# Score products cut by the causal quarter in a fused RWKV-7, windowed attention and convolution kernel

## The chip, the core and the metric

The kernel is one launch on one core of a Trainium2 chip. The metric is the device time of one execution in microseconds, median of three runs. Five engines work side by side and meet through semaphores: TensorE (PE in the profile; its weight loads are PEld), VectorE (DVE), ScalarE (ACT), GpSimd (POOL), and SyncE (SP), which issues most of the weight loads. PE reads SBUF and writes PSUM, which has eight banks of 2 KB per partition.

## What is computed

The reference is one layer: RMS norm, one projection `w_in`, an RWKV-7 recurrence over 16 heads of 64, an attention over windows of 128 with a sink, gates and projections, and a feed-forward part with a short convolution. The change lies in the recurrence:

```
def step(S, inp):
    r_t, w_t, k_t, v_t, aa_t, bb_t = inp
    sa = jnp.einsum('bhvk,bhk->bhv', S, aa_t)
    S = S * w_t[:, :, None, :] + sa[..., None] * bb_t[:, :, None, :] + v_t[..., None] * k_t[:, :, None, :]
    y_t = jnp.einsum('bhvk,bhk->bhv', S, r_t)
    return S, y_t
...
mean = jnp.mean(y, axis=-1, keepdims=True)
var = jnp.mean(jnp.square(y - mean), axis=-1, keepdims=True)
y = (y - mean) * lax.rsqrt(var + GN_EPS)
y = y.reshape(B, T, RWKV_DIM) * lnx_w.astype(f32) + lnx_b.astype(f32)
bonus = jnp.sum(rh * kh * r_k.astype(f32), axis=-1, keepdims=True) * vh
y = (y + bonus.reshape(B, T, RWKV_DIM)) * g.astype(f32)
```

T is 512 tokens. The step is linear in S, so the kernel works on chunks of 128 tokens with matrices of scores, which are zero where the key's token comes after the query's.

## The kernel before

The recurrence runs in eight **pairs** of heads, n = 0 to 7, 64 partitions for each head. Each engine has its instructions in an order written out by hand; semaphores with running counts join them. For one pair PE does, in this order:

- `scores`: per chunk j (four) and head h (two), one matmul with the 64x128 weights `bp` (the beta keys) or `kp` (the kappa keys) and the 256 columns of `ar` (alpha beside r) as moving operand. Every plain f32 matmul leaves two records in the trace, so each matrix has 16. Two chunks of one head fill one PSUM bank. VectorE's `masked` brings each bank to SBUF with a predicated copy through the triangle `causal`, to `gb` for the beta part and `gk` for kappa, and `g_ready` counts the eight copies. A memset of one column stands ahead of each copy and carries its wait.
- `norm_var(d)`, d = n-1: sums for the variance of the pair before, and its bonus rows. ScalarE takes the root (`deviation`, `std_ready`), PE turns it (`turned_var`), VectorE's `deviations` makes a reciprocal and spreads it over `ysq` (`vex_ready`), and PE turns that back (`turned(6, ysq)`, `rstd_ps`).
- `turned(2, ...)`, `turned(3, bp)` and `turned(1, kp)`: values, beta and kappa to token rows, in banks that earlier scores held.
- `invert`: the triangular system of each chunk and head is inverted by doubling, seven levels, 0 to 6. A level is a product on PE into v (`v_ps`), a masked copy on VectorE, a second product (`y_ps`) and an add on VectorE. It works on `n1`, ScalarE's f16 copy of the alpha columns of `gb` (`score_copy`), and VectorE starts `xx` from `n1` (`x_start`). GpSimd's `remainder` forms n2 = gb - n1, which is read after the last level.
- `scan(n)`: the state goes from chunk to chunk.

PE never has nothing to do: between these steps it takes **fillers**, three f32r matmuls of 512 columns each, of the gate and key projections. The tables `FILL`, `FILL_FIRST` and `FILL_LAST` say how many at which place ("scores", "centred", "tokens", (level, "masks") and so on). 24 fillers are three projection tiles per pair. Their weights are split in two on VectorE: `weights` (the whole tile, 1024 columns) and `weights_half` (512 columns, at levels 1, 2, 4 and 5).

GpSimd's queue in a pair: `bonus_product`, a store of gates, `odd_columns`, `remainder`, `bonus_back` (a store of `brow`, then two loads into z), `key_norms_in` (two loads of `kqn`, after `rstd_ps`), and the product of the loaded bonus with the values (`product_ready`, which VectorE wants at level 4). For pair 0 GpSimd also sets `gk` to zero once `ops_ready` says that the attention's scratch is free, and `cleared` counts that.

## Time and profile before

| what | us |
|---|---|
| median of three runs | 1024.72 (1024.06 to 1024.76) |
| the profiled execution | 1024.05 |
| its span | 1022.3 |
| PE busy in the span | 1011.7 |
| first scores, pair 0 | at 213.6 |
| last scores, pair 7 | at 498.1 |

Read it so: the pairs stand between 213.6 and about 525 us, each some 40.6 us long. The rest of the span is projection, attention and feed-forward work that the diff leaves alone. The granted PE clock is full speed in all 40 slices.

### The profile page before, as it was taken

To read this page: it belongs to the slowest core of one execution; us is meant where nothing else is said; L and a number is where in the kernel's file an instruction comes from. 1 tells how busy PE (TensorE), PEld (TensorE's weight loads), DVE (VectorE), ACT (ScalarE), POOL (GpSimd) and SP (SyncE) were. 2 spreads that over 40 slices of the span, in tenths; PEclk is the share of its full clock that TensorE was granted. 3 is DMA by queue.
4 is the path that set the end of the run, shared out by engine and by line. 5 is a ranking of instruction groups with operands and counts; after the bars stand their busy time and mean duration, and the time that the engine had idled before them with its cause. 6 is when DMAs were issued, how large, how long until landed. Compare 5 with 4: busy or idle time off the path is not lost.

```text
span 1022.3 us, 18746 instructions
## 1 busy us (share of the span) xinstructions
PE 1011.7 (99%) x7106; PEld 806.3 (79%) x7106; DVE 738.1 (72%) x1233; ACT 516.2 (50%) x869; POOL 224.4 (22%) x298
## 2 busy tenths in 40 slices
PE   8999999999999999999999999999999999999997
PEld 7888888777777777777777888888888888888886
DVE  5224667788988888888877565367767777789786
ACT  6435756844435445345453322264455444467744
POOL 7642355330221422413210554000000000000000
PEclk9999999999999999999999999999999999999999
DMA  6874456331303313214255867613233333337662
GB/s 187 233 236 153 132 191 215 94 76 43 86 25 74 86 63 87 61 60 120 93 164 153 238 234 258 198 40 103 85 102 92 95 100 103 92 114 226 203 189 113
DMA packets 161291, 133.25 MB, mean 130 GB/s; under 512 B 32729, under 2 KB 137735, under 8 KB 161223
## 3 DMA queue, kind: packets, MB, share of 16 engines
q1 hardware_dynamic: 147687, 88.41, 29.7%
q0 software_dynamic: 13520, 43.90, 13.9%
q8 instruction: 47, 0.77, 0.3%
q14 instruction: 21, 0.17, 0.0%
q10 hardware_dynamic: 16, 0.00, 0.0%
HBM read 111.83 MB, written 20.45 MB: 129 GB/s over the span
## 4 chain that ended last, share of the span: by engine, by line
PE 94%; DVE 2%; DMA 1%; issue 1%; ACT 1%; POOL 0%; SPq 0%; DVEq 0%; POOLq 0%; ACTq 0%
PE ps L2090 14%; PE ps L2093 14%; PE ps L2092 14%; PE ps L2046 6%; PE ps L2048 5%; PE ps L2047 5%; PE ps L2677 3%; PE ps L2678 3%; PE ps L2679 3%; PE ps L2291 3%; PE ps L2425 2%; PE ps L2232 2%; PE ps L2613 1%; PE ps L2611 1%; PE ps L2612 1%; PE ps L2374 1%
## 5 line engine op out<-in xcount | busy, mean ns | idle before, releaser
L1357 DVE TENSOR_TENSOR wlo<-raw,whi 128x1024 fp32r<-128x1024 f32 x106 | 140.1, 1322 | 125.9 <-ACT whi L893 108.0
L893 ACT ACTIVATE whi<-raw 128x1024 fp32r<-128x1024 f32 x116 | 122.6, 1057 | 127.0 <-PE ps L2093 116.0
L2090 PE MATMUL ps<-xnh,whi 128*128 128x512 f32 x336 | 130.7, 389 | 0.0
L2092 PE MATMUL ps<-xnl,whi 128*128 128x512 f32 x336 | 130.7, 389 | 0.0
L2093 PE MATMUL ps<-xnh,wlo 128*128 128x512 f32 x336 | 130.7, 389 | 0.0
L2046 PE MATMUL ps<-xh,whi 128*128 128x512 f32 x192 | 89.5, 466 | 0.0
L2090 PE MATMUL ps<-xh,whi 128*128 128x512 f32 x224 | 88.3, 394 | 0.0
L2092 PE MATMUL ps<-xl,whi 128*128 128x512 f32 x224 | 87.3, 390 | 0.0
L2093 PE MATMUL ps<-xh,wlo 128*128 128x512 f32 x224 | 87.2, 389 | 0.0
L2048 PE MATMUL ps<-xh,wlo 128*128 128x512 f32 x192 | 76.1, 396 | 0.0
L2047 PE MATMUL ps<-xl,whi 128*128 128x512 f32 x192 | 75.3, 392 | 0.0
L2090 PEld LDWEIGHTS ps<-xnh,whi 128*128 128x128 f32 x336 | 63.1, 188 | 13.2
L2092 PEld LDWEIGHTS ps<-xnl,whi 128*128 128x128 f32 x336 | 63.1, 188 | 13.2
L2093 PEld LDWEIGHTS ps<-xnh,wlo 128*128 128x128 f32 x336 | 63.1, 188 | 13.0
L1093 ACT ACTIVATE xx<-ps 128x256 f16<-128x256 f32 x96 | 32.1, 381 | 69.1 <-PE ps L2331 68.3
L2090 PEld LDWEIGHTS ps<-xh,whi 128*128 128x128 f32 x224 | 42.0, 188 | 10.1 <-issue 0.8
L2093 PEld LDWEIGHTS ps<-xh,wlo 128*128 128x128 f32 x224 | 42.1, 188 | 8.9
L2092 PEld LDWEIGHTS ps<-xl,whi 128*128 128x128 f32 x224 | 42.1, 188 | 8.4
L1879 DVE TENSOR_TENSOR sq<-ps,rs 128x512 f32<-128x512 f32 x44 | 30.4, 691 | 23.5 <-PE ps L2093 18.5
L745 POOL TENSOR_TENSOR z<-z,kmod 128x512 f32<-128x512 f32 x8 | 16.2, 2025 | 126.2 <-DVE kp L1488 126.2
L2048 PEld LDWEIGHTS ps<-xh,wlo 128*128 128x128 f32 x192 | 36.0, 188 | 8.3
L1608 DVE TENSOR_TENSOR yy<-ps,yy 128x256 f16<-128x256 f32 x96 | 36.2, 419 | 8.6 <-PE ps L2374 8.3
(430 smaller groups left out, 2454.6 us busy)
## 6 DMA issues: line engine op xcount, KB each, us to landing
raw<-in_w_in SPq DMA_DIRECT2D x108, 256.0 KB, 3.3
raw<-in_w_up SPq DMA_DIRECT2D x88, 256.0 KB, 3.0
wrow<-in_w_down POOLq DMA_DIRECT2D x22, 512.0 KB, 5.1
raw<-weight_scratch SPq DMA_DIRECT2D x44, 256.0 KB, 3.4
raw<-in_w_down SPq DMA_DIRECT2D x32, 256.0 KB, 2.9
weight_scratch<-wrow POOLq DMA_DIRECT2D x11, 512.0 KB, 3.1
gates_scratch<-gst POOLq DMA_DIRECT2D x16, 256.0 KB, 3.2
raw<-in_w_proj_b SPq DMA_DIRECT2D x16, 256.0 KB, 4.2
```

What stands on the lines that cost most here:

```text
L893: act.activation(flat(whi[:, hb]), flat(raw[:, b]), ACT.Copy).then_inc(w_hi, 1)
L1093: act.activation(dst, src, ACT.Copy).then_inc(x_ready, 1)
L1357: dve.tensor_tensor(flat(lo[:, hb]), flat(raw[:, b]), flat(hi[:, hb]).bitcast(F32), ALU.subtract).then_inc(w_lo, 1)
L1608: dve.tensor_tensor(yg, low_half(ps[2 * g][:, :], lv), yg, ALU.add)\
L2046: pe.matmul(o, whi[:, hb, k, :], self.hi(k), start=k == 0, stop=False)
L2047: pe.matmul(o, whi[:, hb, k, :], self.lo(k), start=False, stop=False)
L2048: ins = pe.matmul(o, wlo[:, hb, k, :], self.hi(k), start=False, stop=k == KT - 1)
L2090: pe.matmul(ps[bank][:, :], whi[:, hb, k, :], hi(k), start=first and k == 0, stop=False)
L2092: pe.matmul(ps[bank][:, :], whi[:, hb, k, :], lo(k), start=False, stop=False)
L2093: ins = pe.matmul(ps[bank][:, :], wlo[:, hb, k, :], hi(k), start=False, stop=last and k == kn - 1)
L2291: ins = pe.matmul(ps[SCORE_BANK[f + h]][:, (j - j0) * 2 * C: (j - j0 + 1) * 2 * C], src[hs, j * C:(j + 1) * C], ar[hs, 1 - n % 2, j, :], s ...
L2677: pe.matmul(o, h_hi, hi[:, cols], start=start, stop=False)
```

## The change

The matrices of scores of a chunk are cut in the middle of the token axes. Keys 0 to 63 against queries 0 to 63 are the **early** quadrant; the columns of queries 64 to 127 are the **late** half, for all 128 keys. The quadrant of late keys and early queries is zero and is left out.

- PE: 16 early matmuls with 64x64 weights and 128 columns; even chunks land in the upper 64 partitions of the bank, odd ones in the lower. Then 16 late matmuls with 64x128 weights and 128 columns. The banks are 2 and 3 for early, 0, 1, 4 and 5 for late.
- VectorE: four early copies of 64 partitions for both matrices at once, with one memset ahead of the first, two late copies of beta, the centring of the values (`value_tokens`), two late copies of kappa. `gb` and `gk` become views of one tile, `gg`. In pair 0 the early copies wait for `cleared` 2, since they write both.
- `turned_var` goes behind the turning of values and beta. The filler at "scores" is gone and "centred" has two. `deviations` moves into `invert`: on VectorE behind the level 0 copies, on PE behind the first product of level 1.
- ScalarE's `score_copy` waits for six copies in place of four.
- GpSimd: `bonus_back` goes ahead of `remainder`, and `remainder` waits for `x_start` too.

```diff
+EARLY_BANK = (2, 3)
+LATE_BANK = ((0, 1), (4, 5))
...
+        gg = take("gg", [P, NT, 2, 2, 2, C])
+        gb, gk = (gg[:, 2 * i:2 * i + 2].rearrange("p x e h q t -> p (x e) h (q t)")
+                  for i in range(2))
...
             def remainder(n):
                 pool.wait_ge(n1_ready, n + 1)
+                pool.wait_ge(x_start, n + 1)
...
                 odd_columns(n)
+                bonus_back(n - 1)
                 remainder(n)
-                bonus_back(n - 1)
...
             def score_copy(n):
-                act.wait_ge(g_ready, n * 8 + 4)
+                act.wait_ge(g_ready, n * 8 + 6)
...
+            def early_masked(n, h, e):
+                if n == 0:
+                    dve.wait_ge(cleared, 2)
+                dve.wait_ge(g_ps, n * 8 + 4)
+                predicated(gg[0:HD, :, e, h, :, 0:C // 2],
+                           two_parts(causal[0:HD, :], slice(0, C // 2)),
+                           ps[EARLY_BANK[h]][e * HD:(e + 1) * HD, :]
+                           .rearrange("p (x q t) -> p x q t", x=NT, q=2),
+                           None if h or e else 0)
...
+                    if lv == 0 and d is not None:
+                        deviations(d)
...
-                for f in range(6):
-                    masked(n, f)
-                deviations(n - 1)
-                for f in range(6, 8):
-                    masked(n, f)
+                masked(n, 0)
                 value_tokens(n)
+                masked(n, 1)
                 invert(n, n - 1, n < PAIRS - 1)
...
+                for i, src in enumerate((bp, kp)):
+                    for jj in range(2):
+                        o = (2 * i + jj) * C
+                        for e in range(2):
+                            j = 2 * jj + e
+                            for h, hs in enumerate(rows):
+                                ins = pe.matmul(ps[EARLY_BANK[h]][e * HD:(e + 1) * HD, o:o + C]
+                                                .rearrange("p (q t) -> p q t", q=2),
+                                                src[hs, j * C:j * C + HD], both(hs, j, slice(0, HD)),
+                                                start=True, stop=True)
+                                if i and jj:
+                                    ins.then_inc(g_ps, 1)
+                late(0)
+                late(1)
                 if d is not None:
                     norm_var(d)
-                fill("scores")
-                if d is not None:
-                    turned_var(d)
-                pe.wait_ge(g_ready, n * 8 + 3)
+                pe.wait_ge(g_ready, n * 8 + 2)
                 turned(2, z[:, n + 16, :]).then_inc(tok_ps, 1)
                 pe.wait_ge(g_ready, n * 8 + 4)
                 turned(3, bp).then_inc(tok_ps, 1)
                 if d is not None:
-                    deviations(d)
+                    turned_var(d)
                 fill("centred")
-                pe.wait_ge(g_ready, n * 8 + 8)
+                pe.wait_ge(g_ready, n * 8 + 6)
                 turned(1, kp).then_inc(tok_ps, 1)
...
+                    if lv == 1 and d is not None:
+                        deviations(d)
                     fill((lv, "masks"))
```

PE's order at the start of a pair's scores, before (`gb,up` is the end of the pair before, `z,rkcols` the bonus sums):

```order
L2291 MATMUL ps<-ar,bp 128x256 [waits ops_ready]
L2291 MATMUL ps<-ar,bp 128x256 x7
L2291 MATMUL ps<-ar,kp 128x256 x4
L2291 MATMUL ps<-ar,kp 128x256 [waits g_ready]
L2291 MATMUL ps<-ar,kp 128x256 x3
L2226 MATMUL ps<-ysq,meancols 32x128 [waits y_scaled,ysq_ready]
```

And now:

```order
L2331 MATMUL ps<-ar,bp 64x128 [waits ops_ready]
L2331 MATMUL ps<-ar,bp 64x128 x7
L2331 MATMUL ps<-ar,kp 64x128 x8
L2318 MATMUL ps<-ar,bp 128x128 x8
L2318 MATMUL ps<-ar,kp 128x128 x8
L2251 MATMUL ps<-ysq,meancols 32x128 [waits y_scaled,ysq_ready]
```

Twice the matmuls, each of half the columns, and no wait inside them.

VectorE's order at the end of the copies and the start of the inversion, before (`n_95` is `n1`, `v_96` is `v1`):

```order
L1532 COPY_PREDICATED gk<-causal,ps 128x2x256
L1520 RECIPROCAL ystd<-ps 128x8 [waits std_ps]
L1507 COPY ysq<-ystd 128x512 [waits dve_chain]
L1531 MEMSET carrier 128x1 [waits g_ps]
L1532 COPY_PREDICATED gk<-causal,ps 128x2x256
L1531 MEMSET carrier 128x1 [waits g_ps]
L1532 COPY_PREDICATED gk<-causal,ps 128x2x256
L1497 TENSOR_REDUCE vsum<-ps 128x8 [waits tok_ps]
L1499 SCALAR_TENSOR_TENSOR vp<-vsum,ps 128x512 [waits dve_chain]
L1582 TENSOR_TENSOR xx<-n_95,first_level 128x1024 [waits n1_ready,rk_product]
L1597 TENSOR_TENSOR yy<-ps,level_mask 128x256 [waits v_ps] x2
L1597 TENSOR_TENSOR v_96<-ps,level_mask 128x128x2 [waits v_ps] x2
```

And now:

```order
L1502 SCALAR_TENSOR_TENSOR vp<-vsum,ps 128x512 [waits dve_chain]
L1531 MEMSET carrier 128x1 [waits g_ps]
L1532 COPY_PREDICATED gg<-causal,ps 128x4x2x64
L1531 MEMSET carrier 128x1 [waits g_ps]
L1532 COPY_PREDICATED gg<-causal,ps 128x4x2x64
L1608 TENSOR_TENSOR xx<-n_95,first_level 128x1024 [waits n1_ready,rk_product]
L1623 TENSOR_TENSOR yy<-ps,level_mask 128x256 [waits v_ps] x2
L1523 RECIPROCAL ystd<-ps 128x8 [waits std_ps]
L1510 COPY ysq<-ystd 128x512 [waits dve_chain]
L1623 TENSOR_TENSOR v_96<-ps,level_mask 128x128x2 [waits v_ps] x2
```

The reciprocal and the spread copy stood ahead of the last two copies of kappa, and now stand behind `xx` and the level 0 copies.

GpSimd's order in the same pair, before:

```order
L752 COPY yy<-ident 128x512 [waits ops_ready]
L738 TENSOR_TENSOR n_97<-gb,n_95 128x1024 [waits n1_ready]
L814 DMA bonus_scratch<-brow 128x128 [waits std_ready]
L817 DMA z<-bonus_scratch 64x4x128 [waits brow_stored]
L817 DMA z<-bonus_scratch 64x4x128
L808 DMA kqn<-key_scratch 64x4x128 [waits rstd_ps]
L808 DMA kqn<-key_scratch 64x4x128
L850 TENSOR_TENSOR z<-z 128x512 [waits bonus_in]
```

And now:

```order
L755 COPY yy<-ident 128x512 [waits ops_ready]
L817 DMA bonus_scratch<-brow 128x128 [waits std_ready]
L820 DMA z<-bonus_scratch 64x4x128 [waits brow_stored]
L820 DMA z<-bonus_scratch 64x4x128
L741 TENSOR_TENSOR n_97<-gg,n_95 128x1024 [waits x_start,n1_ready]
L811 DMA kqn<-key_scratch 64x4x128 [waits rstd_ps]
L811 DMA kqn<-key_scratch 64x4x128
L853 TENSOR_TENSOR z<-z 128x512 [waits bonus_in]
```

The subtraction (`n_97`, which is n2) moved behind the three bonus transfers and has a second wait.

## Rows read from the trace of the kernel before

**Rows 1.** The page: busy time of each engine, share of the span, instructions.

```profile
PE 1011.7 (99%) x7106; PEld 806.3 (79%) x7106; DVE 738.1 (72%) x1233; ACT 516.2 (50%) x869; POOL 224.4 (22%) x298
```

**Rows 2.** Timeline, PE, pair 5: start us, us, engine, line, operation, shapes, count.

```profile
416.86 2.00 PE L2291 MATMUL ps<-ar,bp 64*128 64x256 f32 x16
...
420.54 0.42 PE L2226 MATMUL ps<-ysq,meancols 128*32 128x128 f32 x8
420.79 0.40 PE L2226 MATMUL ps<-z,rkcols 128*32 128x128 f32 x8
...
422.95 0.66 PE L2232 MATMUL ps<-ident,ysq 128*128 128x128 f32 x4
423.37 0.48 PE L2046 MATMUL ps<-xh,whi 128*128 128x512 f32 x1
...
428.41 0.41 PE L2374 MATMUL ps<-v,xx 128*128 128x64 f16 x8
...
430.71 0.41 PE L2374 MATMUL ps<-v,xx 128*128 128x64 f16 x8
```

**Rows 3.** Timeline, PE, a score product of the attention stage.

```profile
84.36 1.16 PE L2176 MATMUL ps<-kb,qc 64*128 64x128 f32 x16
```

**Rows 4.** Timeline, DVE, pair 5.

```profile
418.03 0.75 DVE L1532 COPY_PREDICATED gb<-causal,ps 128x512 f32<-128x512 uint32 x1 [0.29 <-issue]
418.66 0.76 DVE L1532 COPY_PREDICATED gb<-causal,ps 128x512 f32<-128x512 uint32 x1
...
422.47 0.43 DVE L1507 COPY ysq<-ystd 128x512 f32<-128x512 f32 x1
...
424.13 0.66 DVE L1497 TENSOR_REDUCE vsum<-ps 128x8 f32<-128x512 f32 x1
...
425.43 0.69 DVE L1582 TENSOR_TENSOR xx<-n,first_level 128x1024 f16<-128x1024 f16 x1
426.03 0.78 DVE L1597 TENSOR_TENSOR yy<-ps,level_mask 128x256 f16<-128x256 f32 x2
...
429.41 0.68 DVE L1569 TENSOR_TENSOR wlo<-raw,whi 128x512 fp32r<-128x512 f32 x1
430.01 0.75 DVE L1597 TENSOR_TENSOR v<-ps,level_mask 128x256 f16<-128x256 f32 x2
```

**Rows 5.** Timeline, POOL, pair 5.

```profile
422.82 2.15 POOL L738 TENSOR_TENSOR n<-gb,n 128x1024 f16<-128x1024 f32 x1 [2.65 <-ACT n L1073]
...
427.01 1.26 POOL L817 DMA_DIRECT2D z<-bonus_scratch  x2 [1.55 <-DMA bonus_scratch<-brow]
428.26 1.25 POOL L808 DMA_DIRECT2D kqn<-key_scratch  x2
...
432.60 1.29 POOL L850 TENSOR_TENSOR z<-z 128x512 f32<-128x512 f32 x1 [3.09 <-DMA z<-bonus_scratch]
```

**Rows 6.** Timeline, pair 0, POOL and DVE.

```profile
215.26 1.88 POOL L829 MEMSET gk<- 128x2048 f32 x1
...
220.43 2.17 POOL L738 TENSOR_TENSOR n<-gb,n 128x1024 f16<-128x1024 f32 x1
...
221.67 1.49 DVE L1582 TENSOR_TENSOR xx<-n,first_level 128x1024 f16<-128x1024 f16 x1
```

**Rows 7.** Timeline, late in the attention stage, POOL and DVE.

```profile
187.93 1.81 POOL L797 MEMSET gb<- 128x2048 f32 x1 [0.89 <-ACT vc L983]
...
188.57 1.19 DVE L1414 TENSOR_SCALAR nmx<-mx 128x8 f32<-128x8 f32 x1
```

**Rows 8.** Timeline, pair 0 and pair 1: PE and DVE.

```profile
218.95 0.60 PE L2232 MATMUL ps<-ident,bp 128*128 128x128 f32 x4
...
253.87 2.00 PE L2291 MATMUL ps<-ar,bp 64*128 64x256 f32 x16
...
255.33 0.74 DVE L1532 COPY_PREDICATED gb<-causal,ps 128x512 f32<-128x512 uint32 x1
...
265.69 0.41 PE L2374 MATMUL ps<-v,xx 128*128 128x64 f16 x8
```

63 lines of the change are left out of this document (36 added, 27 removed).

## The prediction

> **What bounds the kernel now.** First the page: PE is busy 1011.7 of 1022.3 us [rows 1]. Nothing else comes near, so the kernel gets shorter only where PE has less work, and longer by every wait put into PE's queue. Then the timeline of one pair, since the other seven repeat it. I take pair 5, count from its first score product at 416.86, and call that zero. The scores last until the variance sums at 420.54, 3.68 us; the level 1 update (L2374) starts at 428.41, so at 11.55 [rows 2]. All that the diff moves lies between these two marks or hangs on VectorE's and GpSimd's queues in that stretch [rows 4, 5]. So I ask when the level 1 update starts now. PE has a filler at almost every place, and the fillers keep their number; a wait that outlasts them is lost for good.
>
> **PE's own work.** Before: 32 score records, 3.68 us [rows 2]. Late: 32 records of 128 columns in the form of the attention's product, 16 in about 1.0 to 1.16 us [rows 3], so some 2.0 us. Early: 32 records of 128 columns on quarters of the array. No row shows a 64x64 product. The nearest is the variance sum, also 128 columns and four parts of the array side by side: 8 records in 0.25 us (420.54 to 420.79) [rows 2], so 32 in 1.0 us. If two run at a time and not four, they cost half of today's scores, 1.84 us. I take 1.0, by the row with four parts at work. Scores then last 3.0 to 3.1 us, 0.6 us less in each of eight pairs. The merged filler saves one start, about 0.1 us. If PE waited for nobody, this would be worth 8 x 0.7 = 5.6 us. It does wait, as follows.
>
> **VectorE's chain.** The first early copy needs all early products. The last group of 8 begins at 0.75 and ends 0.42 later, at 1.17; the copy follows 0.24 us on, as I read the 418.03 start behind the first products. So it starts at 1.41 (now 1.17) [rows 2, 4]. The eight copies have as many elements as before. Copies start 0.63 us apart (418.03, 418.66) and take 0.75 each [rows 4]. The four early ones read partitions 0 and 64 in turn with no memset between; no row has that, so their step lies between 0.63 (overlapped as now) and 0.75 (one after another), and I take the middle, 0.69, as no row is nearer to either. Two late copies of 0.63 and 0.65, the two steps of `value_tokens` 1.30 (424.13 to 425.43), two more copies 1.28 [rows 4]: `xx` starts at 1.41 + 2.76 + 1.28 + 1.30 + 1.28 = 8.03 and ends 0.69 later, at 8.72. It started at 8.57 before. The three memsets that fall away are 0.06 us each and lie under the copies: nothing.
>
> On this step the Trainium skill has a rule, in "VectorE: DVE Perf Modes", section "Two Vector instructions with no wait between them": an instruction whose input starts in another group of 32 partitions than the last one read there is held until the earlier ones have finished. By it the step would be the long one; by the rows alone it is open. No run here shows it yet.
>
> **Where it turns: the spread copy meets the subtraction.** `deviations` now stands behind `xx` and the level 0 copies, and PE takes its result at level 1. GpSimd's `remainder` (2.15 us) [rows 5] now waits for `x_start`, so it starts just as `xx` ends: 8.72 + 0.08 = 8.80, until 10.95. The level 0 copies start 0.60 after `xx`, last 0.67, then the reciprocal 0.24; the spread copy wants to start at 9.54, in the middle of the subtraction. Can they run together? Two rows say no. In pair 0 `xx` took 1.49 us and not 0.69, beside the same subtraction, which ended at 222.60; `xx` ended at 223.16 [rows 4, 6]. And a VectorE instruction with one input, 8 elements wide, took 1.19 us and ended at 189.76, when GpSimd's memset ended at 189.74 [rows 7]. The spread copy moves 512 f32 elements in 0.43 us, where a predicated copy of as many takes 0.75 [rows 4]: it runs in a faster mode, the kind of instruction I expect to be shut out. It would then end about 0.30 after the subtraction (as `xx` did, 0.13 less than its length), at 11.25. PE's turning of `ysq` starts at 11.30, then 0.42 to the filler's start (422.95 to 423.37) and 0.79 for the filler: the level 1 update starts at 12.51 and not at 11.55 [rows 2]. PE's own path would have brought it to the turning at about 9.6: it stands still for 1.7 us, more than all that the scores save.
>
> The skill's page "SBUF — State Buffer", section "Who interferes with whom", gives the reason and names the class: a copy of f32 from SBUF to SBUF can take the port pair shared with GpSimd, and the second to issue blocks fully until the first is done. The two rows above agree with it, 1.49 and 1.19 us; for this very copy no row shows it.
>
> Cost: pairs 3 to 7, 0.96 each, 4.8 us. In pairs 1 and 2 VectorE has one more instruction and started its copies at 255.33 - 253.87 = 1.46 already; their update stood at 265.69 - 253.87 = 11.82 [rows 8] and goes to 12.56: 0.74 each, 1.5 us.
>
> **A second collision.** `key_norms_in` waits for `rstd_ps`, which the turning at 11.30 gives at 12.0. Its two transfers take 1.25 [rows 5], then the bonus product (1.29) runs from 13.3 to 14.6. Its data are there: the loads into z are issued from about 6.5 and the product started 5.6 after that issue (427.01 to 432.60) [rows 5], so at 12.1. VectorE's first half split of weights starts 1.00 after the update (428.41 to 429.41) [rows 2, 4], at 13.5, and has two SBUF inputs, as `xx` has. It would be shut out until 14.6 and end at 15.15 in place of 14.2. The level 2 masks behind it come 0.95 late; level 2's update, which stands 0.70 behind their start (430.01 to 430.71) with nothing to spare, moves by about 0.9. That hits pairs 1 to 6, 5.4 us; pair 7 has no key norms to load. The order of the two is a matter of 0.2 us, so this term is the least sure. Bounds: 0 and 0.95 a pair.
>
> **Pair 0.** Its early copies wait until GpSimd has cleared `gk`, 215.26 + 1.88 = 217.14 [rows 6]; before, the first copy needed only `gb`. The fourth copy then ends at 217.2 + 3 x 0.69 + 0.75 = 220.0, and PE turns beta at 220.1 in place of 218.95 [rows 8], with one filler (0.8) still to come that stood ahead of it. Cost 1.9 us; with steps of 0.63, 1.7. ScalarE's score copy is later too, but PE meets it behind three fillers. In this pair `xx` gains, 0.69 for 1.49, hidden under the fillers of level 0.
>
> **GpSimd's order.** Bonus rows go some 3.7 us earlier and are wanted at level 4: nothing. n2 ends at 10.95, wanted after level 6: nothing. ScalarE's copy for `n1` ends near 6.8 for a filler that PE reaches at about 6.7: a few hundredths, and inside the wait at the turning.
>
> **Sum.** 4.8 + 1.5 + 5.4 + 1.9 = 13.6 us. The profiled execution was 1024.05 with a span of 1022.3, so 1.75 us lie outside the span, untouched; it stands 0.67 below the median. 1024.72 + 13.6 = **1038.3 us**.
>
> **The rivals.**
> 1. *Blocked, but no second collision.* The half split starts before the product and GpSimd waits. 13.6 - 5.4 = 8.2: 1032.9; with steps of 0.63, 1031. For it: the order is decided by 0.2 us. Chance 0.22.
> 2. *The spread copy runs beside the subtraction.* Then the turning follows VectorE's own chain, 9.54 + 0.43 + 0.05 = 10.02, the update stands at 11.23: 0.32 less than before in five pairs, 0.54 less in two, 1.9 lost in pair 0, so -0.8: 1023.9. With steps of 0.63 the update comes 0.24 earlier and pair 0 loses 1.7: -2.7, **1022.1, faster**. It decides from where the spread copy takes its usual 0.43 us in pairs 1 to 7. For it: no row shows a spread copy beside GpSimd, and its source is a broadcast; against it, the two blocked rows. Chance 0.15, half of it faster, half within 0.2%.
> 3. *Quarters of the array run two at a time.* The first early copy then starts 0.84 later, all behind it too, except in pair 0, which waits for GpSimd anyway: about +5.8, 1044.1. Against it: four parts are at work in the variance sums. Chance 0.07.
> 4. Something else that I don't see, either way: 0.06.
>
> The forecast itself has 0.50. **Range**: the steps of 0.75 add 1.9, to 1040.2, and a part of rival 3 goes to 1043; below, rival 1 with short steps is 1031, and between it and rival 2 lie mixtures (blocked in part, or rival 2 with the second collision), so I go down to 1026. A difference of 0.2%, 2 us, is about what a measurement can tell here. Faster: half of rival 2 and a third of the last case, 0.09. Same: 0.09. Slower: 0.82.
>
> **What the changed profile will show.** Early records of x32 in about 1.0 us, scores 3.0 to 3.1 us long, each pair. The spread copy (L1510) at 1.5 to 1.7 us in place of 0.43, ending with GpSimd's subtraction (L741), and PE's turning of `ysq` right behind it; if it stands at 0.43, rival 2 holds. Half splits (L1595) of 1.5 us in pairs 1 to 6; if all are 0.68, rival 1. In pair 0 the first early copy at 217.2 with PE idle before it. `xx` at 0.69 in all pairs. PE's busy time should fall or stay while the span grows. I am wrong altogether if PE reaches the level 1 update sooner than 11.5 us after its first score product.

## The result and the profile after

| | before | after |
|---|---|---|
| median, us | 1024.74 (4 runs, 1024.06 to 1025.93) | 1045.16 (4 runs, 1043.99 to 1049.69) |
| span of the profiled execution, us | 1022.3 | 1043.6 |
| its own time, us | 1024.05 | 1045.36 |
| ratio | | 1.0209, interval 1.0197 to 1.0222 |

The change makes the kernel 2.1% slower, 20.4 us. Direction and mechanism are those of the prediction; the forecast of 1038.3 was 6.9 us too low, and the measured time lies above the range that ended at 1043. So does the fastest execution of after, 1043.99 us with a granted clock of 1.000 over its span; the slowest, 1049.69, had 0.989.

The page of after, the lines that answer to [rows 1]:

```profile
span 1043.6 us, 19242 instructions
PE 1012.1 (97%) x7362; PEld 808.3 (77%) x7362; DVE 755.0 (72%) x1209; ACT 516.9 (50%) x869; POOL 225.1 (22%) x298
```

PE's busy time is the same (1011.7 before), and the span is 21.3 us longer. So PE stands still now. What it waits for, after, in the view of PE's waits (engine and line, what released it, us in total, times, longest us), the three longest but for a load at the start:

```profile
PE ps L2257 <- DVE ysq L1510: 12.4, 7, 2.1
PE ps L2415 <- DVE v L1623: 4.2, 6, 0.8
PE ps L2257 <- DVE gg L1532: 3.4, 4, 2.0
```

None of the three was in the trace of before. The first is the turning of the spread copy, seven times; the second is the level 2 update behind a late half split; the third is mostly pair 0. Now pair 5, where the first score product stands at 430.27. Timeline, PE, after:

```profile
430.27 0.67 PE L2331 MATMUL ps<-ar,bp 64*64 64x128 f32 x16
...
433.29 0.43 PE L2251 MATMUL ps<-ysq,meancols 128*32 128x128 f32 x8
...
439.86 0.41 PE L2390 MATMUL ps<-yy,n 128*128 128x64 f16 x8
441.97 0.66 PE L2257 MATMUL ps<-ident,ysq 128*128 128x128 f32 x4 [1.70 <-DVE ysq L1510]
...
443.17 0.41 PE L2415 MATMUL ps<-v,xx 128*128 128x64 f16 x8
...
446.43 0.62 PE L2415 MATMUL ps<-v,xx 128*128 128x64 f16 x8 [0.81 <-DVE v L1623]
```

The last line once more in two narrow windows, since it is two groups of four, one for each of the two mask copies:

```profile
446.43 0.29 PE L2415 MATMUL ps<-v,xx 128*128 128x64 f16 x4 [0.81 <-DVE v L1623]
...
446.76 0.29 PE L2415 MATMUL ps<-v,xx 128*128 128x64 f16 x4
```

Timeline, DVE, after, same pair:

```profile
431.53 0.72 DVE L1532 COPY_PREDICATED gg<-causal,ps 64x512 f32<-64x512 uint32 x1 [0.38 <-issue]
...
432.28 2.28 DVE L1532 COPY_PREDICATED gg<-causal,ps 64x512 f32<-64x512 uint32 x3
...
438.48 0.68 DVE L1608 TENSOR_TENSOR xx<-n,first_level 128x1024 f16<-128x1024 f16 x1
...
439.97 1.95 DVE L1510 COPY ysq<-ystd 128x512 f32<-128x512 f32 x1
...
444.17 1.86 DVE L1595 TENSOR_TENSOR wlo<-raw,whi 128x512 fp32r<-128x512 f32 x1
445.96 0.74 DVE L1623 TENSOR_TENSOR v<-ps,level_mask 128x256 f16<-128x256 f32 x2
```

The second of these two masks in a narrow window:

```profile
446.29 0.41 DVE L1623 TENSOR_TENSOR v<-ps,level_mask 128x256 f16<-128x256 f32 x1
```

Timeline, POOL, after, same pair:

```profile
438.21 1.25 POOL L820 DMA_DIRECT2D z<-bonus_scratch  x2 [2.84 <-DMA bonus_scratch<-brow]
439.48 2.14 POOL L741 TENSOR_TENSOR n<-gg,n 128x1024 f16<-128x1024 f32 x1
...
442.93 1.24 POOL L811 DMA_DIRECT2D kqn<-key_scratch  x2 [1.30 <-PE ps L2257]
444.17 1.30 POOL L853 TENSOR_TENSOR z<-z 128x512 f32<-128x512 f32 x1
```

Read the three together. The spread copy, 0.43 us before [rows 4], takes 1.95 and ends at 441.92, 0.30 behind GpSimd's subtraction (441.62). PE has nothing left from 440.27 on and turns `ysq` at 441.97. The half split, 0.68 before [rows 4], starts in the same hundredth as the bonus product, takes 1.86 and ends at 446.03, 0.56 behind it. The update of level 2 comes 3.26 behind that of level 1, where it was 2.30 [rows 2]. It also takes 0.62 in place of 0.41: its first four products start 0.06 behind the first mask (446.37), and the other four wait for the second mask, which ends at 446.70. Before, PE came to the update only when the first mask had been ready for 0.28 us, and the second wait hardly showed. The summary of the spread copy's line over the whole of after (duration in ns, least, median and most; first and last start) says that seven of eight were like this, and the one behind the last pair was not:

```profile
L1510 DVE COPY ysq<-ystd x8: 426/1992/2348, 267.3 to 564.7; 128x512 f32<-128x512 f32 x8
```

The 21.3 us by pair, from the first score product of a pair to that of the next (pair 7: to its last update):

| pair | before | after | more | of it at the level 1 update | at level 2 | at level 3 |
|---|---|---|---|---|---|---|
| 0 | 40.23 | 43.78 | 3.55 | 3.55 | 0 | 0 |
| 1 | 40.86 | 43.11 | 2.25 | 1.07 | 0.97 | 0.21 |
| 2 | 40.89 | 43.43 | 2.54 | 1.35 | 0.96 | 0.22 |
| 3 | 40.62 | 42.94 | 2.32 | 1.19 | 0.96 | 0.22 |
| 4 | 40.62 | 43.36 | 2.74 | 1.58 | 0.96 | 0.22 |
| 5 | 40.64 | 43.14 | 2.50 | 1.35 | 0.96 | 0.21 |
| 6 | 40.62 | 43.90 | 3.28 | 1.73 | 1.57 | 0 |
| 7 | 23.99 | 26.11 | 2.12 | 1.58 | 0.34 | 0.21 |

The columns add up to 13.4, 6.7 and 1.3 us; the forecast had 8.2 (1.9 + 1.5 + 4.8), 5.4 and nothing. The last two columns are one loss: the first is what the first half of the level 2 update lost, and the second what its other half lost on top, behind the second mask. Together they are 1.17 to 1.18 us in pairs 1 to 5.

Pair 0. Timeline, PE, after:

```profile
218.72 0.66 PE L2257 MATMUL ps<-ident,z 128*128 128x128 f32 x4 [1.99 <-DVE gg L1532]
220.24 0.81 PE L2257 MATMUL ps<-ident,bp 128*128 128x128 f32 x4 [0.86 <-DVE gg L1532]
220.70 0.77 PE L2071 MATMUL ps<-xh,whi 128*128 128x512 f32 x1
221.27 0.63 PE L2072 MATMUL ps<-xl,whi 128*128 128x512 f32 x1
221.69 0.63 PE L2073 MATMUL ps<-xh,wlo 128*128 128x512 f32 x1
```

Windows of after (start:end, length, busy us of PE, of its weight loads, of DVE, ACT and POOL, then PEclk, the granted clock as a share of 2.4 GHz, the DMA engines' share, GB/s):

```profile
218.00:225.00 7.00, 5.42 (x22) 4.37 (x23) 6.60 (x14) 2.35 (x3) 2.52 (x6) 0.76 0.49 74
...
484.00:492.00 8.00, 6.50 (x62) 4.86 (x63) 6.40 (x11) 2.46 (x5) 3.68 (x4) 0.79 0.48 56
```

Beta is turned at 220.24, 6.59 behind the first score product where it was 5.31 [rows 8], as forecast (220.1; the copies wait for the memset). But the filler products that follow start 0.57 and 0.42 apart and not 0.23: TensorE ran at its lower level, 1.2 GHz, until about 224, after two stretches of idle time, 1.99 and 0.86 us. In before the same window had a clock of 1.00. Pair 6 shows the same after a wait of 2.10 us: 0.79 in its window, 1.00 before. Pairs 4 and 7, with waits of 1.94 and 1.92 us, show no filler at the lower level.

### The profile page after: what moved, and what is told of

The parts are those of the page before. It is cut to its first block, busy times and chain, and to the rows that moved or that the text cites. A ratio compares the mean times of both kernels' runs of the same rounds, so it can differ in the third digit from the quotient of the medians.

```text
span 1043.6 us, 19242 instructions
## 1 busy us (share of the span) xinstructions
PE 1012.1 (97%) x7362; PEld 808.3 (77%) x7362; DVE 755.0 (72%) x1209; ACT 516.9 (50%) x869; POOL 225.1 (22%) x298
## 3 DMA queue, kind: packets, MB, share of 16 engines
q0 software_dynamic: 13520, 43.90, 14.4%
## 4 chain that ended last, share of the span: by engine, by line
PE 84%; DVE 10%; issue 3%; DMA 1%; ACT 1%; POOL 0%; SPq 0%; DVEq 0%; POOLq 0%; ACTq 0%
PE ps L2115 14%; PE ps L2117 14%; PE ps L2118 14%; PE ps L2071 5%; PE ps L2073 4%; PE ps L2072 4%; PE ps L2718 3%; PE ps L2720 3%; PE ps L2719 3%; DVE gg L1532 2%; DVE ysq L1510 1%; PE ps L2415 1%; PE ps L2653 1%; PE ps L2654 1%; PE ps L2652 1%
## 5 line engine op out<-in xcount | busy, mean ns | idle before, releaser
L1532 DVE COPY_PREDICATED gg<-causal,ps 64x512 f32<-64x512 uint32 (+1 forms) x64 | 45.6, 735 | 4.8 <-issue 1.9
L2118 PEld LDWEIGHTS ps<-xh,wlo 128*128 128x128 f32 x224 | 42.0, 188 | 8.9
L1636 DVE TENSOR_TENSOR yy<-ps,yy 128x256 f16<-128x256 f32 x96 | 36.2, 419 | 13.4 <-PE ps L2415 12.6
```

What stands on the lines that cost most here:

```text
L1532: dve.copy_predicated(dst, mask.bitcast(U32).unsqueeze(1) .to_broadcast([mask.shape[0], NT, 2, C // 2]), scores)\
L1636: dve.tensor_tensor(yg, low_half(ps[2 * g][:, :], lv), yg, ALU.add)\
L2118: ins = pe.matmul(ps[bank][:, :], wlo[:, hb, k, :], hi(k), start=False, stop=last and k == kn - 1)
```

## The experiments

Three questions were open. Is it the meeting on the two engines' time line that makes the spread copy and the half split long, or the copy's new place, or the split of the copies? What does each cost? And what is the rest of pair 0? In the rows of an experiment the line numbers are its own. Kernels that ran together share the runs of the kernel before, whose median lay between 1024.41 and 1024.74 each time.

### Only GpSimd held back: `gate_only`

```diff
-                remainder(n)
                 if n < PAIRS - 1:
                     pool.wait_ge(rstd_ps, n)
                     key_norms_in(n + 1)
+                pool.wait_ge(w_half, 2 * n + 1)
                 pool.wait_ge(bonus_in, 32 * n)
                 pool.tensor_tensor(z[:, n + 7, :], z[:, n + 15, :], z[:, n + 7, :], ALU.mult)\
                     .then_inc(product_ready, 1)
+                pool.wait_ge(w_lo, N_FILL + 3 * n + 2)
+                remainder(n)
```

> The changed kernel with GpSimd alone held back: the bonus product waits until the first half split of level 2 is done, and the subtraction stands behind the product and waits for the third split, so that neither runs while VectorE spreads 1/std or makes the first half split. The split copies, the late spread copy and pair 0 stay as in the change. Theory (the two collisions between GpSimd and the spread copy and half split are the loss of pairs 1 to 7): spread copy 0.43 instead of 1.75 to 2.35, half splits 0.68 instead of 1.25 to 1.86, level 1 update at 11.3 to 11.6 (now 12.7 to 13.3), pairs 1 to 6 at 40.4 to 40.9 (now 42.9 to 43.9), pair 0 unchanged at 43.8; whole 1026 to 1029. Rival (the extra late copies and the spread copy's late place lengthen VectorE's own chain, and the collisions only fill time that it would wait anyway): pairs stay above 42, whole above 1037.

Measured: 1027.16 us (10 runs, 1025.24 to 1028.73), ratio 1.0027 [1.0017, 1.0036]; span 1024.2. The expected time, and the expected rows but for two: pair 0 took 42.23 and not 43.8 (its clock did not fall, see further down), and the second half split, at level 2, met the product in pairs 4 to 7 and took 0.80 to 1.30. Timeline, DVE, `gate_only`, pair 5 (first score product at 418.80):

```profile
428.50 0.43 DVE L1512 COPY ysq<-ystd 128x512 f32<-128x512 f32 x1
...
431.19 0.68 DVE L1597 TENSOR_TENSOR wlo<-raw,whi 128x512 fp32r<-128x512 f32 x1
```

Timeline, POOL, `gate_only`:

```profile
432.54 1.28 POOL L853 TENSOR_TENSOR z<-z 128x512 f32<-128x512 f32 x1 [1.37 <-DMA z<-bonus_scratch]
434.45 2.14 POOL L741 TENSOR_TENSOR n<-gg,n 128x1024 f16<-128x1024 f32 x1 [0.63 <-DVE wlo L1597]
```

Waits of PE, `gate_only`:

```profile
PE ps L2259 <- DVE ysq L1512: 1.3, 7, 0.2
```

Nothing of PE's or VectorE's work was touched, and 18.0 us are gone; by the two traces 19.4, of which 1.55 is the clock in pair 0. PE's wait for the spread copy falls from 12.4 to 1.3 us, pairs 1 to 6 take 40.4 to 40.8. The two collisions are the loss of pairs 1 to 7: shown. This kernel also answers for pair 0, further down.

### The spread copy back at its early place: `dev_early`

```diff
                 masked(n, 0)
+                deviations(n - 1)
                 value_tokens(n)
                 masked(n, 1)
                 invert(n, n - 1, n < PAIRS - 1)
...
-                    if lv == 0 and d is not None:
-                        deviations(d)
```

> One edit: VectorE's reciprocal and spread copy go back ahead of the centring of the values, where GpSimd has no computing instruction; PE still turns ysq at level 1. Shared way into SBUF: the copy takes 0.43 us again, xx starts 0.65 later, PE waits at most 0.4 us for the level 0 copies, and the half split of level 1 starts before the bonus product: about 2.4 us a pair less, 1028. Chain on VectorE alone: the work on VectorE is the same, so the time stays near 1045.

Measured: 1032.37 us (1031.68 to 1033.15), ratio 1.0076 [1.0059, 1.0092]; span 1030.7. All spread copies take 0.43 us, and the level 1 update stands at 11.6 to 11.8 behind the first score product. GpSimd's subtraction still stands behind `xx` and disturbs nothing now. The second collision came and went with the place of the product. Timeline, DVE, `dev_early`, pair 3:

```profile
354.97 2.22 DVE L1595 TENSOR_TENSOR wlo<-raw,whi 128x512 fp32r<-128x512 f32 x1
```

Timeline, POOL, `dev_early`, pair 3:

```profile
355.33 1.31 POOL L853 TENSOR_TENSOR z<-z 128x512 f32<-128x512 f32 x1
```

In pairs 1 and 3 the half split took 2.22 us and ended 0.55 behind the product (pairs of 42.36 and 42.18); in pair 2 the product began 0.65 behind its start, in pairs 4 to 6 more than 0.9, and those pairs took 40.6 to 40.8. So a product a few tenths of a microsecond earlier or later costs 1.5 us or nothing.

### GpSimd's order as before: `undo_pool`

```diff
                 pool.wait_ge(n1_ready, n + 1)
-                pool.wait_ge(x_start, n + 1)
...
-                bonus_back(n - 1)
                 remainder(n)
+                bonus_back(n - 1)
```

> One edit: GpSimd's part undone, the subtraction again ahead of the bonus transfers and without its wait for x_start. Shared way into SBUF: now xx is shut out by about 0.6 us, the spread copy is free at 0.43, and the bonus product comes long after the half split of level 1: 2 us a pair less, about 1030. If instead the splitting of the scores itself costs the time, it stays near 1045.

Measured: 1031.49 us (1030.63 to 1032.7), ratio 1.0064 [1.0047, 1.0081]; span 1031.0. Timeline, DVE, `undo_pool`, pair 5:

```profile
432.10 1.36 DVE L1607 TENSOR_TENSOR xx<-n,first_level 128x1024 f16<-128x1024 f16 x1
...
434.28 0.43 DVE L1509 COPY ysq<-ystd 128x512 f32<-128x512 f32 x1
```

Timeline, POOL, `undo_pool`:

```profile
430.76 2.15 POOL L740 TENSOR_TENSOR n<-gg,n 128x1024 f16<-128x1024 f32 x1 [3.58 <-ACT n L1075]
```

The subtraction is ahead of the spread copy again, which takes 0.43; now `xx` is the one that is shut out, 1.36 us in place of 0.69, until 0.55 behind the subtraction. That is why the change holds the subtraction back: the split makes `n1` ready earlier, and the subtraction would sit beside `xx`. But 0.7 us there cost less than 1.5 at the spread copy. All half splits take 0.68.

### Both back, only the split copies left: `split_alone`

The two edits above together.

> The changed kernel with both of these undone (VectorE's spread copy early again, GpSimd's order and wait as before): the split of the scores and what hangs on it alone. No instruction is shut out for longer than 0.2 us, the half splits are all 0.68; pairs 1 to 7 take 40.6 us as before, though PE has 0.65 us less work in each, since VectorE's copies decide when level 1 can start. What is left above 1024.7 is pair 0, 3.5 to 4.7 us: 1028 to 1030. If PE's smaller work comes through, 1024.

Measured: 1030.12 us (1028.14 to 1031.02), ratio 1.0044 [1.003, 1.0058]; span 1029.3. Pairs 3 to 6 take 40.77 to 40.81, 0.15 to 0.19 longer than before although the scores are 0.65 us shorter: VectorE's chain gives the gain back (PE's waits for the level 0 copies: 2.5 us in seven pairs). There are eight copies a pair as before, but the first starts 0.09 later, four of the steps are long (`copy_order`, below), and `xx` takes 0.80 in place of 0.68, since it starts before the subtraction ends. What each of these costs alone was not measured. Pair 0 takes 45.04. The split of the products alone brings nothing and costs 4.8 us in pair 0, clock included.

### The two moves, each alone, in the kernel before

`pool_on_before` (GpSimd's bonus transfers first, the subtraction held until `xx`):

```diff
                 pool.wait_ge(n1_ready, n + 1)
+                pool.wait_ge(x_start, n + 1)
...
-                remainder(n)
                 bonus_back(n - 1)
+                remainder(n)
```

> The kernel before with GpSimd's part of the change alone (bonus transfers first, the subtraction after xx). The spread copy stands ahead of xx there, so nothing on VectorE that wants the shared way runs beside the subtraction. Collision theory: the time stays at 1024.7 within 2 us, unless the bonus product, now earlier, meets the half split of level 1 (then up to 6 us more). If the new order of GpSimd is dear in itself, through its later subtraction, about 10 us more.

Measured: 1024.41 us (10 runs), ratio 1.0000 [0.9991, 1.001]; span 1022.6. No change: the spread copy sits ahead of the subtraction, 0.43 us long. The product meets the half split here too, but it is the product that waits. Timeline, POOL, `pool_on_before`, pair 5 (the half split runs from 429.79 for 0.68):

```profile
426.64 2.14 POOL L739 TENSOR_TENSOR n<-gb,n 128x1024 f16<-128x1024 f32 x1 [0.84 <-DVE xx L1583]
...
429.99 1.64 POOL L851 TENSOR_TENSOR z<-z 128x512 f32<-128x512 f32 x1
```

`dev_on_before` (only the spread copy and PE's turning of it moved; the first two pieces are VectorE's, the last two TensorE's):

```diff
+                    if lv == 0 and d is not None:
+                        deviations(d)
...
-                for f in range(6):
+                for f in range(8):
                     masked(n, f)
-                deviations(n - 1)
-                for f in range(6, 8):
-                    masked(n, f)
...
-                if d is not None:
-                    deviations(d)
                 fill("centred")
...
+                    if lv == 1 and d is not None:
+                        deviations(d)
                     fill((lv, "masks"))
```

> The kernel before with the move of the reciprocal and spread copy alone (VectorE behind the level 0 copies, PE at level 1); GpSimd's order as before. The subtraction is over by 8.1 us of the pair, the spread copy comes at about 9: it takes 0.43 us, and the time stays within 2 us of 1024.7. If the move is dear in itself, because PE waits for a longer chain, 5 us or more above.

Measured: 1022.23 us (10 runs, 1021.73 to 1023.24), ratio 0.9976 [0.9966, 0.9985]; span 1020.4. A gain of 2.4 us, the best kernel of all. Timeline, DVE, `dev_on_before`, pair 5 (first score product at 416.00):

```profile
423.60 1.05 DVE L1582 TENSOR_TENSOR xx<-n,first_level 128x1024 f16<-128x1024 f16 x1
...
425.46 0.43 DVE L1507 COPY ysq<-ystd 128x512 f32<-128x512 f32 x1
```

Timeline, POOL, `dev_on_before`:

```profile
421.94 2.15 POOL L738 TENSOR_TENSOR n<-gb,n 128x1024 f16<-128x1024 f32 x1 [2.63 <-ACT n L1073]
```

The spread copy is off the chain that leads to `xx`, so the level 1 update comes at 11.20 and not 11.55 [rows 2]. The subtraction ends at 424.09, ahead of the copy: they don't meet. It meets `xx` instead (1.05 in place of 0.69), and the pair gains even so. Of the two halves of the move one is worth nothing alone and the other 2.4 us; in the changed kernel, together, they put the two instructions side by side. Both together in the kernel before were not run.

### The product ahead of the key norms: `prod_first`

```diff
+                pool.wait_ge(bonus_in, 32 * n)
+                pool.tensor_tensor(z[:, n + 7, :], z[:, n + 15, :], z[:, n + 7, :], ALU.mult)\
+                    .then_inc(product_ready, 1)
                 if n < PAIRS - 1:
                     pool.wait_ge(rstd_ps, n)
                     key_norms_in(n + 1)
-                pool.wait_ge(bonus_in, 32 * n)
-                pool.tensor_tensor(z[:, n + 7, :], z[:, n + 15, :], z[:, n + 7, :], ALU.mult)\
-                    .then_inc(product_ready, 1)
```

> One edit: the bonus product goes ahead of the key norm loads on GpSimd. Shared way into SBUF: in pairs 1 to 3, whose bonus rows land early, the half split of level 1 is 0.68 us again and not 1.86; in pairs 4 to 6, whose store of bonus rows takes 3 us, the product still meets it in part. About 4.5 us less, 1040. If the long half split has another cause (its weights, PE), its length stays 1.86 us and the time 1045.

Measured: 1041.52 us (1040.64 to 1042.27), ratio 1.0167 [1.015, 1.0184]; span 1038.9. In pairs 1 to 3 the level 2 update is back at 2.30 behind that of level 1, and the pairs take 1.15 to 1.2 us less than in after. In pairs 4 to 6 it is not. There the z loads wait 2.7 to 3.4 us for the bonus rows' store (3.36 in pair 5), and the product then waits another 2.0 to 2.3 for the loads to land, so it still starts only 0.60 and 0.31 us ahead of the half split in pairs 4 and 6. In these two the first half of level 2 is still 0.3 and 0.6 us late; in pair 5 the spread copy takes 2.46 us, PE idles for 2.21, and the next filler products start 0.58 and 0.43 apart, at the lower clock. Right for three pairs of six.

### One reciprocal out of PSUM in place of reciprocal and spread copy: `psum_recip`

```diff
-                chain(dve.reciprocal(by_token(ystd[:, :]), by_token(ps[6][:, P:2 * P])))
-                spread(ysq, ystd).then_inc(vex_ready, 1)
+                dve.reciprocal(ysq[:, :].rearrange("p (j h v) -> p j h v", j=NT, v=HD),
+                               by_token(ps[6][:, P:2 * P]).unsqueeze(3)
+                               .to_broadcast([P, NT, 2, HD])).then_inc(vex_ready, 1)
```

> One edit to the changed kernel: VectorE's reciprocal and spread copy become one reciprocal of 512 elements that reads PSUM and no SBUF; GpSimd's queue is untouched. If the spread copy is shut out by GpSimd's subtraction because both want the shared way into SBUF, the new instruction takes about 0.7 us beside the subtraction, PE's idle of 1.5 to 2.1 us ahead of turning ysq shrinks to about 0.3, and the time falls from 1045 by 10 us or more, to about 1034; the half split may then come ahead of the bonus product and free up to 6 us more (1028). If the wait at the turning is only a long chain on VectorE, the time stays within 2 us of 1045.

Measured: 1061.3 us (1059.62 to 1062.32), ratio 1.0352 [1.0335, 1.037]; span 1060.6. Timeline, DVE, `psum_recip`, pair 1:

```profile
312.12 3.35 DVE L1523 RECIPROCAL ysq<-ps 128x512 f32<-128x512 f32 x1
```

The expected 0.7 us was a miss. The operation takes 3.33 to 3.35 us in all seven pairs, though GpSimd's subtraction (2.1 us) runs beside it in each, and 3.35 behind the last pair, where GpSimd does nothing. So this operation, which reads PSUM, is not shut out at the very place where the spread copy is; but it is dearer than the blocked copy, and PE waits 22.9 us for it. The time says nothing about the theory, the lengths do.

### Pair 0: fillers ahead of the first wait, `p0_fill`

```diff
                 if d is not None:
                     norm_var(d)
+                fill("scores")
                 pe.wait_ge(g_ready, n * 8 + 2)
...
-            FILL_FIRST = {**FILL, "centred": 3, (3, "update"): 1}
+            FILL_FIRST = {**FILL, "scores": 3, "centred": 0, (3, "update"): 1}
```

> Only in pair 0: the three fillers stand ahead of the first wait for a copy (ahead of value head's turning) instead of behind the beta turnings. Nothing else of the changed kernel is touched. Theory (pair 0 lost 3.55 us: 1.9 of it idle time of TensorE behind the late memset, the rest because its granted clock fell after that idle time and everything to 225 ran at the lower level): the fillers cover 0.7 us of the idle stretch with work; if that keeps the clock at 1.00 in 218 to 225, pair 0 takes 42.0 to 42.4 instead of 43.78 and the whole 1043.4 to 1043.8; pairs 1 to 7 keep their 42.9 to 43.9. Rival (all 3.55 us are waits for VectorE and the clock is without effect): pair 0 shortens by at most the 0.7 us of the three fillers that stood behind the wait, 43.1, whole 1044.5 or more.

Measured: 1045.19 us (1044.27 to 1045.48), ratio 1.0197 [1.0182, 1.0213]; span 1043.8. Pair 0 takes 43.42, not 42.0 to 42.4. The times are on the rival's side (43.1 or more, 1044.5 or more), but they don't speak for it, since the clock fell here too. The long idle stretch is gone, but three shorter ones take its place, and the granted clock is 0.89 in 218 to 225, with the low level from 223.4 to 226.7. Timeline, PE, `p0_fill`:

```profile
220.94 0.66 PE L2257 MATMUL ps<-ident,bp 128*128 128x128 f32 x4 [0.83 <-DVE gg L1532]
222.34 0.66 PE L2257 MATMUL ps<-ident,kp 128*128 128x128 f32 x4 [0.74 <-DVE gg L1532]
223.43 0.80 PE L2071 MATMUL ps<-xh,whi 128*128 128x512 f32 x1 [0.43 <-ACT n L1076]
```

The price of the clock came out of `gate_only`, whose pair 0 has the change's edits and the same waits of PE, and in whose profiled execution the clock did not fall. Timeline, PE, and window, `gate_only`:

```profile
219.30 0.66 PE L2259 MATMUL ps<-ident,z 128*128 128x128 f32 x4 [1.99 <-DVE gg L1534]
220.81 0.66 PE L2259 MATMUL ps<-ident,bp 128*128 128x128 f32 x4 [0.86 <-DVE gg L1534]
```

```profile
218.00:225.00 7.00, 4.84 (x33) 3.84 (x33) 6.84 (x15) 2.79 (x4) 2.98 (x5) 1.00 0.54 100
```

Its pair 0 takes 42.23: 2.0 us more than before, where the prediction had 1.9. With the clock at 0.76 (after) it takes 43.78, and in `dev_early`, `undo_pool` and `split_alone`, at 0.63, 0.61 and 0.69, it takes 44.89, 44.99 and 45.04. PE's waits for the early copies add up to 3.4 us in each of these. So the waits cost 2.0 us of the pair, and the clock 1.5 to 2.8 on top. The same kernel doesn't pay it in every execution: over the ten runs of `gate_only` the mean clock of the span goes from 0.999 (1025.24 us) down to 0.996 (1028.73 us). What decides it from run to run stays open.

### The order of the early copies: `copy_order`

```diff
-                    for h in range(2):
-                        for e in range(2):
+                    for e in range(2):
+                        for h in range(2):
                             early_masked(n, h, e)
...
-                pe.wait_ge(g_ready, n * 8 + 2)
+                pe.wait_ge(g_ready, n * 8 + 3)
```

> The changed kernel with its four early masked copies in the order head 0 and head 1 of one operand, then of the other, in place of both operands of head 0 first; TensorE's first turning waits for the third copy. Theory (a copy that starts on other partitions than the one before takes the longer step, 0.76 us, one on the same partitions 0.63): if the step hangs on a change of start partition alone, the order changes the last three steps' sum of 2.28 us by -0.1 to -0.25 and the subtraction xx starts that much earlier; the whole moves by less than 1.5 us, 1043.7 to 1045.2, since the turning waits for the spread copy behind GpSimd's subtraction, and not for xx. Rival (the step of 0.76 is that of every pair of copies that follow each other at once): 2.28 unchanged, whole 1045.2 within 0.5. Against both: pair 0 may lose 0.7 us more, since its first turning then waits for one copy more.

Measured: 1044.28 us (1043.86 to 1045.62), ratio 1.0195 [1.018, 1.0211]; span 1042.2. Timeline, DVE, `copy_order`, pair 5:

```profile
430.71 0.73 DVE L1532 COPY_PREDICATED gg<-causal,ps 64x512 f32<-64x512 uint32 x1 [0.38 <-issue]
...
431.35 2.11 DVE L1532 COPY_PREDICATED gg<-causal,ps 64x512 f32<-64x512 uint32 x3
```

The first copy and the second write and read the same partitions, and their step is 0.64; in after they change partitions, and the step is 0.75. The next three take 2.11 in place of 2.28. In both kernels every step to another start partition is 0.74 to 0.79, the one from the last early copy to the first late one too, and the others are 0.62 to 0.66. So it is the change of start partition that makes a step long, as expected. Pairs 1, 2, 3 and 5 are 0.26 to 0.31 shorter, the others scatter with the collisions; the whole can't be told from after at this precision.

### Everything mended, and once too much: `tuned1` and `tuned2`

`tuned1` is `gate_only`, `p0_fill` and `copy_order` in one, with pair 0's two late beta copies made ahead of its early ones, since they don't need the memset; TensorE's first two turnings then wait for the fifth and sixth copy there:

```diff
             def masked(n, i):
+                if n == 0 and i == 0:
+                    for h in range(2):
+                        late_masked(n, 0, h)
```

> The changed kernel with GpSimd put where it meets nothing: bonus product behind the half split of level 1, subtraction behind the half split of level 2; early copies in the order of partitions 0, 0, 64, 64; in pair 0 the late beta copies ahead of the early ones and three fillers ahead of the first wait. Collision theory: spread copy 0.43, half splits 0.68, level 1 update at about 11.2 of the pair and not 12.9, pair 0 costs 0.5 to 1 us and not 3.6, PE's clock stays up: 1022 to 1023, faster than both kernels. If something else holds the pairs back, it stays above 1028.

Measured: 1022.92 us (10 runs, 1021.9 to 1023.96), ratio 0.9981 [0.9971, 0.999]; span 1021.8. Pair 0 takes 40.54 (before 40.23, after 43.78) with the clock at 1.00; pairs 1 to 3 take 40.16 to 40.37, pairs 4 to 6 40.27 to 40.63, where the second half split met the product (1.05 to 1.37 us). The changed kernel's layout with GpSimd kept out of the way is 0.2% faster than before, at the edge of what can be told; it does not beat the simple `dev_on_before`.

`tuned2` moves one wait of it:

```diff
-                pool.wait_ge(w_half, 2 * n + 1)
+                pool.wait_ge(w_half, 2 * n + 2)
```

> The last mended version with one wait moved: the bonus product waits for the second half split of level 2 in place of the first. Theory (in pairs 4 to 6 of that version the second half split took 1.15 instead of 0.68 us because the product ran beside it, and levels 2 and 3 came 0.15 to 0.5 us late): half splits all 0.68, pairs 4 to 6 at 40.15 to 40.2 (were 40.27 to 40.63), whole 1021.9 to 1022.4, against 1022.92 for that version and 1022.23 for the kernel before with only the spread copy moved. Rival (the late product now delays the subtraction and through it the masks of level 3 or the next pair's odd columns, or the differences came from the bonus store and not from the product): pairs 1 to 3 longer than 40.4, whole 1022.9 or more.

Measured: 1046.84 us (5 runs, 1045.76 to 1048.02), ratio 1.0216 [1.0202, 1.023]; span 1045.1. The rival side, and far beyond the price that I gave it. Levels 1 to 4 do come on time. But `w_half` counts only every other split, so this wait is for the third and not the second: the step of my expectation that failed is that reading. Timeline, POOL, `tuned2`, pair 5:

```profile
448.52 1.27 POOL L853 TENSOR_TENSOR z<-z 128x512 f32<-128x512 f32 x1 [6.76 <-DVE wlo L1601]
449.76 2.13 POOL L741 TENSOR_TENSOR n<-gg,n 128x1024 f16<-128x1024 f32 x1
```

Timeline, DVE, `tuned2`:

```profile
449.83 2.61 DVE L1581 SCALAR_TENSOR_TENSOR ysb<-ysb,par,z 128x512 f32<-128x512 f32 x1 [0.73 <-POOL z L853]
```

`with_bonus` waits for the product (0.73), starts 0.07 behind the subtraction, and is shut out by it: 2.61 us in place of 0.74. PE waits up to 2.2 us for the masks behind it, in seven pairs, 13.7 us, and the filler products behind that start 0.40 apart at first (453.41, 453.81) in place of 0.23: the lower clock again. Pairs 1 to 6 take 42.7 to 44.3. A third collision of the same kind, made by moving one wait.

## Why the prediction was right in kind and too low

**Right.**
- Scores take 3.02 us (433.29 - 430.27), forecast 3.0 to 3.1: the 32 early records take 1.04 of them, forecast 1.0 with four quarters at work and 1.84 with two. Rival 3 is out.
- The spread copy is shut out and ends 0.30 us behind the subtraction, forecast 0.30. With the rule in the Trainium skill, "SBUF — State Buffer", section "Who interferes with whom", the trace agrees: 0.43 us alone, 1.75 to 2.35 beside the subtraction. Rival 2, the only faster case, is out; `dev_early` and `gate_only` show that the 0.43 comes back as soon as they don't meet.
- The half split meets the product, in every pair forecast to have it. Rival 1 is out. (The +0.96 at level 2 looks like the 0.9 that was forecast, but it is only the first half of the loss; see below.)
- Pair 0's waits: 2.0 us, forecast 1.9 (`gate_only`).

**Wrong, by size.** The sum was 13.6 us and the span grew by 21.3.
- *The turning of `ysq`, forecast at 11.30 in every pair, stands at 11.52 to 12.09*: 3.6 us over seven pairs. Two terms failed. The step of the early copies, taken as the middle 0.69, is 0.76 (2.28 us for three), and the step to the first late copy is as long; since the first copy starts at 1.26 and not at 1.41, `xx` starts only 0.18 later than forecast. By the Trainium skill, "VectorE: DVE Perf Modes", section "Two Vector instructions with no wait between them", it would be the long step, and the trace agrees (0.74 to 0.79 against 0.62 to 0.66); I had given either side equal weight. And the subtraction does not start "just as `xx` ends": in pair 5 it starts 0.41 later than forecast, right behind the second z load, because that load had waited 2.84 us for the bonus rows' store, where [rows 5] showed a wait of 1.55. I had costed the moved transfers at nothing. They stand ahead of the subtraction in GpSimd's queue now, so a delay of theirs is one of the subtraction and of the spread copy behind it. One pair had been read for all: in the trace of before the same wait was 1.54 to 1.55 in pairs 2 to 6, but 1.90 in pair 1 and 2.61 in pair 7. Why it is 2.8 to 3.2 in pairs 4 to 7 of after (1.5 to 1.9 in pairs 1 to 3) is open; with the same order in the kernel before (`pool_on_before`) it was 1.54 in pairs 2 to 6. In pair 2 of after the subtraction starts 0.44 behind the end of `xx`, and about 0.15 in pairs 1 and 3, with no late load to explain it; open too.
- *The second collision, forecast at 0.9, costs 1.17 in pairs 1 to 5*: 1.4 us. The prediction let the key norms go out 0.7 us behind the start of the turning, and they went 0.96 behind it (442.93 - 441.97). So the product starts not 0.2 ahead of the half split but together with it, the half split ends 1.18 late and not 0.95, and with it both masks. The update has two halves: the first had 0.2 us to spare in before, which is why it moved by 0.96, and the second, with next to none, moved by 1.17.
- *Pair 7 was left out of the second collision*, because it "has no key norms to load". Its product runs without them, and its half split still took 1.25 us: 0.55 us.
- *Pair 0, 1.9, took 3.55.* The waits were right; what the prediction left out is that TensorE's clock can fall to 1.2 GHz after such idle time, with the work behind it at half speed. That is 1.55 us here (against `gate_only`, where the same waits left it at 1.00). In pair 6, where the clock fell too, levels 2 and 3 cost 1.57, 0.4 more than in the pairs without it. No row of before could show this, since PE hardly ever stood still there.

Added: 3.55 (the turning) + 1.4 + 0.55 + 0.67 (pair 6, 1.57 for 0.9) + 1.65 = 7.8 us, where 21.3 and 13.6 differ by 7.7. The range failed with them. Its upper end had room for long steps and a part of rival 3, and none for a late store, a late product or the clock; all three went the same way. The clock fell only behind waits of the kind that was forecast; whether the late store has to do with them is not shown.

## What to carry to other kernels

An instruction of VectorE that is moved meets another one of GpSimd, and either can shut the other out: before moving one, lay both engines' timelines side by side at the new place, for the moved instruction and for everything whose start hangs on it. Two moves that are harmless alone in the kernel before (0.0 and -2.4 us) cost 15.0 together in the changed one (1045.16 against 1030.12 for `split_alone`). Put a transfer ahead of an instruction in a queue only with its slowest landing in mind, read from all pairs and not from one. When an engine's work is released in halves, follow the last half: the first may have had time to spare. And where TensorE was never idle, price the first idle time not by its length alone: the lower clock behind it cost another 0.4 to 2.8 us here in some executions, and nothing in others.

## What the runs showed of the hardware

- While GpSimd runs a two-input operation, VectorE's f32 spread copy (0.43 us alone) took up to 2.46 (`prod_first`), a two-input subtraction of 512 f32 elements (0.68) up to 2.22, and a scalar-tensor-tensor with all inputs in SBUF (0.74) 2.61. Masks that read PSUM (`v`, `yy`) kept their 0.41 to 0.46 each. Outside the pairs the trace of before had such meetings already: a split of 1024 columns took 3.00 in place of 1.22 (at 631.29), and a two-input instruction on 512 f32 elements 2.38 in place of 0.69 (at 585.75), both beside transfers and a two-input operation of GpSimd.
- Who waits is not always VectorE. In `dev_early`, pair 3, the half split began 0.36 ahead of the product and was still the one shut out (2.22 us); in `pool_on_before` it began 0.20 ahead in pair 5 and 0.34 in pair 3, kept its 0.68 both times, and the product took 1.64 and 1.48 in place of 1.29. In all three GpSimd was still issuing transfers when the half split began. Where it issued none, as in the kernel before in pair 5, the one that began first kept its length: VectorE's split of a whole tile (at 416.52) 1.22, and GpSimd's bonus product, 0.23 behind it, 2.12 in place of 1.35 (pair 0). What decides in the other cases is open.
- A reciprocal of 512 f32 elements out of PSUM takes 3.34 us, 6.5 ns an element, beside GpSimd's subtraction or without it (`psum_recip`), where a predicated copy of 512 takes 0.73 and the reciprocal of 8 takes 0.18 to 0.21.
- Predicated copies of 64 partitions follow each other every 0.62 to 0.66 us on the same partitions and every 0.74 to 0.79 when the start partition changes (`copy_order`, after).
- The clock: after idle stretches of 1.99 and 0.86 us the products ran at 1.2 GHz for about 3.5 us in one execution (0.76 in that window), and at 2.4 GHz throughout in another with the same two waits (1.00, `gate_only`).
